# Float32r products of 512 columns issued as two of 256 in a two-block transformer kernel

## The chip, the cores and the metric

The kernel runs on one core of one Trainium2 chip. The metric is the device time of one execution in microseconds. Before the change it is 1270.01 us, the median of three runs (1269.93 to 1270.71).

## What is computed

The reference takes 512 tokens of width 1024 and sends them through two blocks, all in float32. The first block has an input projection, a short convolution branch, a gated delta rule branch with 8 heads, two output projections, a mixing projection, and a convolutional feed-forward part of width 2816. The second block has another input projection, an indexer that selects keys for one attention, a forgetting attention, a pooling branch and an output projection. Cut to what matters here, which is the large products:

```python
h = rmsnorm(x, norm_mix_g);  proj = h @ w_in                       # 1024 -> 9232
y_a = short_conv_branch(bg, cg, xv, conv_a_w) @ w_a_out            # 1024 -> 1024
y_b = gdn_branch(q, k, v, z, a, b, ...) @ w_b_out                  # 1024 -> 1024
x = x + (sigmoid(ga) * y_a + sigmoid(gb) * y_b) @ w_o
h = rmsnorm(x, norm_ffn_g)
up = causal_dwconv(h @ w_up, ffn_conv_w)                           # 1024 -> 5632
x = x + (silu(gate) * val) @ w_down                                # 2816 -> 1024
z = rmsnorm(x', norm_g_2) @ w_in_2                                 # 1024 -> 3886
x = x' + concat(pool, dsa, fox) @ w_out_2;  out = rmsnorm(x, final_g_2)
```

## The kernel before, in words

Activations lie transposed in SBUF: features on the 128 partitions, the 512 tokens along the free dimension. A weight matrix is worked off in units. A unit is one block of 128 output columns of one matrix: 128 weight columns by up to 1024 input features, which is 8 tiles of 128 x 128 (the second feed-forward matrix has units of 5 or 6 tiles). SyncE loads the block into one of four buffers `raw`. For accuracy every float32 value is used as a sum of two rounded float32r values: ScalarE writes the rounded block `whi` (L1329), VectorE, or in a late stretch GpSimd, writes the rest `wlo = raw - whi` (L1818, L2756). Both have two buffers, and ScalarE may write one again only when the unit that read it two units ago is done (`unit_done`). The activations have been split the same way into slots of `act_a` and `act_b`.

TensorE runs the units one after another in `unit` (L816 to L837). It first waits for `split_ready`. For each of the kn feature tiles it issues three products into the same PSUM bank `gb[:, b, :]` of 128 x 512 float32: high weights by high activations, low weights by high activations, and high weights by low activations. The weight tile is the stationary operand and the 512 tokens of the slot are the moving one. So a unit of 8 tiles is 24 products. `whole` runs a unit without a pause. With `parts=4` the unit is cut into four parts, and between the parts TensorE issues small steps of the head in work: float32 products and transposes of 128 x 128 or smaller (`key_products` L925, `query_products` L933, `step` L943 to L1016) and, in the second block, those of the written plan (`beside`, L1207 attention scores, L1219 transposes, L1229 attention by values). The order is written out by hand in the loops of `head`, `ups`, `down` and over `Z_UNITS`. Other engines wait for the last product of a unit (`unit_done`) and read the bank.

Not made by `unit` are the thin products of the first projection (L880 to L882, a weight tile of 16 columns by 512 tokens) and the last projection (`products`, L1279, 192 products whose stationary tile is an activation and whose moving operand is 512 weight columns).

Of the kernel before, what the change touches and what calls it, by code (L numbers as in the profile page):

```python
# [5 lines left out]
P = 128  # L6
# [198 lines left out]
def hybrid_block_kernel(nc, x, norm_mix_g, w_in, conv_a_w, gdn_conv_w, gdn_A_log, gdn_dt_bias, gdn_norm_g,  # L205
                        w_a_out, w_b_out, w_o, norm_ffn_g, w_up, ffn_conv_w, w_down, norm_final_g,
                        w_in_2, norm_g_2, pool_w_2, pool_scale_2, fox_bf_2, w_out_2, final_g_2, out):
    with ExitStack() as ctx:
# [85 lines left out]
        def slot(n):  # L294
            return act_a[:, n, :] if n < SLOTS_A else act_b[:, n - SLOTS_A, :]
# [25 lines left out]
        gb = ctx.enter_context(nc.psum_tensor("gb", [P, 4, T], F32))  # L321
# [493 lines left out]
        def _(pe):  # L815
            def unit(n, i, b, k0, rhs_hi, rhs_lo, kn=KD, first=True, last=True, parts=1, ready=None, high=None, packed=False):  # L816


                pe.wait_ge(split_ready, n + 1)
                todo = []  # L820
                for k in range(kn):
                    hi = whi[:, i % 2, k * P:k * P + P]
                    lo = wlo[:, i % 2, k * P:k * P + P]
                    a, c = slot(rhs_hi + k0 + k), slot(rhs_lo + k0 + k)
                    todo += [(hi, a), (hi, c)] if packed else [(hi, a), (lo, a), (hi, c)]
                each = len(todo) // parts
                per = len(todo) // kn
                for m, (l, r) in enumerate(todo):
                    if high and m % per == 0:
                        pe.wait_ge(high[0], high[1] + m // per + 1)  # L830
                    if ready and m % per == (per - 1 if high else 0):
                        pe.wait_ge(ready[0], ready[1] + m // per + 1)
                    ins = pe.matmul(gb[:, b, :], l, r, start=(first and m == 0), stop=(last and m == len(todo) - 1))  # L833
                    if m == len(todo) - 1:
                        ins.then_inc(unit_done, 1)
                    if (m + 1) % each == 0:
                        yield  # L837

            def whole(*a, **k):
                for _ in unit(*a, **k):  # L840
                    pass
# [56 lines left out]
            for r in range((R_END + P - 1) // P):  # L898
                m = min(P, R_END - r * P)
                ins = pe.transpose(gd[:, 1, r * P:r * P + m], prow[0:m, r * P:r * P + P], ident[0:m, 0:m])  # L900
            ins.then_inc(par_turned, 1)
            for m, _ in enumerate(unit(N_B, N_B, 0, 0, YB_HI, YB_LO, parts=4)):
                if m == 0:
                    pe.wait_ge(ab_ready, 1)
                    for c in range(TC):
                        ins = pe.transpose(gd[:, 0, c * P:c * P + AB_COLS], ob[0:AB_COLS, c, :],
                                           ident[0:AB_COLS, 0:AB_COLS])
                    ins.then_inc(ab_turned, 1)
                elif m == 2:
                    pe.wait_ge(par_ready, 2)  # L910
                    norm_spread(0)
# [106 lines left out]
            def head(h, peeled):  # L1018
                for s in range(8):
# [14 lines left out]
                    if peeled:  # L1034
                        u = unit(N_B + 8 * h + s, N_B + s, s % 4, 0, YB_HI, YB_LO, parts=4)
                    else:
                        u = unit(N_B + 8 * h + s, N_B + s, s % 4, 0, H_HI, H_LO, parts=4,
                                 ready=(h_ready, 0) if s == 0 else None)
# [232 lines left out]
            def products(i, c):  # L1271
                n, k = N_W + i, W_ORDER[i]
                hi = act_a[:, MIX_HI + k, c * P:c * P + P]
                lo = act_a[:, MIX_LO + k, c * P:c * P + P]
                for half in range(2):
                    wh = whi[:, n % 2, half * T:half * T + T]
                    wl = wlo[:, n % 2, half * T:half * T + T]
                    for m, (l, r) in enumerate(((hi, wh), (lo, wh), (hi, wl))):
                        ins = pe.matmul(place(c, half), l, r, start=False, stop=(i == KD - 1 and m == 2),  # L1279
                                        skip_group_check=True)  # L1280
                    if i == KD - 1 and (half == 1 or c == TC - 1):
                        ins.then_inc(tile_done, 1)
                return ins
# [16 lines left out]
            for i in range(2, KD - 2):  # L1300
                pe.wait_ge(split_ready, N_W + i + 1)
                pe.wait_ge(m_lo, i + 1)
                for c in range(TC):
                    ins = products(i, c)
# [1490 lines left out]
```

## Time and profile before

| | |
|---|---|
| median of three runs | 1270.01 us |
| span of the profiled execution, first to last instruction | 1268.4 us |
| TensorE products, records and busy time | 6633, 1253.7 us (99%) |
| TensorE weight loads, records and busy time | 6633, 1007.2 us (79%) |
| VectorE, ScalarE, GpSimd busy | 832.6, 578.6, 223.9 us |
| DMA, mean rate | 103 GB/s |

Times are in microseconds unless marked ns. PE is TensorE's products and PEld its weight loads, which overlap the products. L833 is line 833 of the kernel. A group of instructions is told by line, engine, operation, output<-inputs and shape. The recorded duration of a product reaches from its start to its modelled end and overlaps the next product's, so durations of products do not add up to time, and the distance between two starts is the time that a product takes. The profile has no own duration of the execution beside its span; the median of the runs is 1.6 us above it.

### The profile page before, as it was taken

Reading aid. Unit: us, or ns where it says so; the run is one execution under the profiler, and the core shown is the slowest. Engines: PE = TensorE matmul, PEld = TensorE weight load, DVE = VectorE, ACT = ScalarE, POOL = GpSimd, SP = SyncE. Lnnn points to the kernel's source line nnn. Section 1 sums busy time; section 2 is a strip of 40 time slices with the busy share of each in tenths; the row PEclk is TensorE's granted clock in tenths of the full one; section 3 lists DMA queues with packets and bytes.
Section 4 is the critical chain, followed back from the end, with each engine's and each line's share of the span. In section 5 each row is a group of like instructions: output and inputs, shape, how many; then the busy total and the mean of one; then the engine's idle time right before and its main releaser. Section 6 shows DMA issues by size and latency. Waiting matters only on the chain.

```text
span 1268.4 us, 20147 instructions
## 1 busy us (share of the span) xinstructions
PE 1253.7 (99%) x6633; PEld 1007.2 (79%) x6633; DVE 832.6 (66%) x1705; ACT 578.6 (46%) x1049; POOL 223.9 (18%) x476
## 2 busy tenths in 40 slices
PE   8999999999999999999999999999999999999998
PEld 6787878878788788888888888888888767777776
DVE  6978777787676843444477773367765686794743
ACT  5664545545455432223344442244444455666632
POOL 2603314032140400001300000000004124440021
PEclk9999999999999999999999999999999999999999
DMA  6345263453534433333233323433224334333221
GB/s 182 84 117 136 75 155 88 120 124 83 141 94 120 125 92 108 99 99 100 83 100 99 99 73 90 118 100 99 81 79 113 102 108 126 83 84 100 80 70 67
DMA packets 283492, 130.01 MB, mean 103 GB/s; under 512 B 77296, under 2 KB 276271, under 8 KB 283445
## 3 DMA queue, kind: packets, MB, share of 16 engines
q1 hardware_dynamic: 283445, 129.42, 37.3%
q8 instruction: 25, 0.41, 0.1%
q14 instruction: 22, 0.18, 0.0%
HBM read 119.34 MB, written 10.06 MB: 102 GB/s over the span
## 4 chain that ended last, share of the span: by engine, by line
PE 95%; DVE 2%; issue 1%; ACT 1%; DMA 0%; SPq 0%; POOLq 0%; DVEq 0%; POOL 0%; ACTq 0%
PE gb L833 82%; PE gb L1279 2%; PE gd L1279 1%; PE gd L1229 1%; PE gd L1219 1%; PE gd L1207 1%; PE gd L925 1%; PE gd L933 1%; PE gd L1005 1%; PE gd L1016 1%; PE gd L994 0%; PE gd L993 0%; PE gd L1012 0%; PE gb L1207 0%; PE gd L1186 0%
## 5 line engine op out<-in xcount | busy, mean ns | idle before, releaser
L833 PE MATMUL gb<-act_a,whi 128*128 128x512 f32 x2656 | 888.8, 398 | 0.3 <-DVE wlo L1818 0.2
L833 PEld LDWEIGHTS gb<-act_a,whi 128*128 128x128 f32 x2656 | 498.9, 188 | 112.0 <-issue 9.9
L833 PE MATMUL gb<-act_a,wlo 128*128 128x512 f32 x1408 | 548.9, 390 | 0.0
L1818 DVE TENSOR_TENSOR wlo<-raw,whi 128x1024 fp32r<-128x1024 f32 (+1 forms) x197 | 235.8, 1197 | 134.6 <-ACT whi L1329 132.5
L1329 ACT ACTIVATE whi<-raw 128x1024 fp32r<-128x1024 f32 (+1 forms) x210 | 216.1, 1029 | 216.9 <-PE gb L833 191.7
L833 PEld LDWEIGHTS gb<-act_a,wlo 128*128 128x128 f32 x1408 | 265.1, 188 | 48.2 <-issue 0.5
L833 PE MATMUL gb<-act_b,whi 128*128 128x512 f32 x432 | 152.5, 393 | 0.0
L833 PEld LDWEIGHTS gb<-act_b,whi 128*128 128x128 f32 x432 | 81.1, 188 | 17.3 <-DVE qc L2112 0.4
L2711 POOL TENSOR_TENSOR zs<-zs,ca 128x512 f32<-128x512 f32 x3 | 4.2, 1395 | 321.3 <-ACT ca L1332 321.3
L833 PE MATMUL gb<-act_b,wlo 128*128 128x512 f32 x128 | 49.9, 390 | 0.0
L2666 POOL TENSOR_TENSOR Ue<-Ue,elt 128x60 f32<-128x60 f32 (+14 forms) x120 | 45.0, 375 | 9.4
L2676 POOL TENSOR_TENSOR rr<-ss,eps_one 128x4 f32<-128x4 f32 x8 | 1.6, 201 | 234.8 <-DVE ss L2003 234.8
L2663 POOL TENSOR_TENSOR elt<-Ti,Ue 128x60 f32<-128x60 f32 (+14 forms) x120 | 37.6, 314 | 27.9 <-DVE Ti L1939 13.5
L2756 POOL TENSOR_TENSOR wlo<-raw,whi 128x1024 fp32r<-128x1024 f32 x13 | 31.2, 2400 | 23.6 <-ACT whi L1329 23.6
L1424 ACT ACTIVATE ob<-gd,hc 128x128 f32<-128x128 f32 x24 | 8.8, 368 | 54.2 <-DVE Rr L2059 54.2
L2323 DVE TENSOR_TENSOR Yb<-gb,Vt 128x512 f32<-128x512 f32 x22 | 15.2, 691 | 24.7 <-PE gb L833 24.7
L2694 POOL TENSOR_TENSOR zs<-zs,ca 128x512 f32<-128x512 f32 x3 | 5.6, 1857 | 134.3 <-ACT ca L1332 134.3
L2362 DVE TENSOR_TENSOR xT<-xT,gb 128x512 f32 (+1 forms) x16 | 11.0, 687 | 26.9 <-PE gb L833 26.9
L833 PEld LDWEIGHTS gb<-act_b,wlo 128*128 128x128 f32 x128 | 24.1, 188 | 4.5
L2448 DVE MAX8 small<-selb 128x8 f32<-128x256 f32 (+2 forms) x48 | 26.4, 549 | 0.4
L2449 DVE MATCH_REPLACE8 selb<-small,selb 128x256 f32<-128x256 f32 (+2 forms) x48 | 26.0, 543 | 0.0
L2112 DVE SCALAR_TENSOR_TENSOR kc<-gb,hw,kc 128x511 f32<-128x511 f32 (+2 forms) x24 | 18.0, 748 | 7.7 <-ACT kc L1445 7.1
(487 smaller groups left out, 1497.3 us busy)
## 6 DMA issues: line engine op xcount, KB each, us to landing
raw<-in_w_in_dram SPq DMA_DIRECT2D x102, 512.0 KB, 3.7
raw<-in_w_up_dram SPq DMA_DIRECT2D x44, 512.0 KB, 3.6
raw<-in_w_down_dram SPq DMA_DIRECT2D x16, 384.0 KB, 3.1
raw<-in_w_down_dram SPq DMA_DIRECT2D x16, 320.0 KB, 3.0
raw<-in_w_a_out_dram SPq DMA_DIRECT2D x8, 512.0 KB, 4.2
raw<-in_w_b_out_dram SPq DMA_DIRECT2D x8, 512.0 KB, 3.5
raw<-in_w_o_dram SPq DMA_DIRECT2D x8, 512.0 KB, 3.4
raw<-in_w_out_dram SPq DMA_DIRECT2D x8, 512.0 KB, 3.5
```

Of the source, the lines that this page charges most:

```text
L833: ins = pe.matmul(gb[:, b, :], l, r, start=(first and m == 0), stop=(last and m == len(todo) - 1))
L925: ins = pe.matmul(gd[:, 3, c * P:c * P + P], KT[:, c, :], KT[:, c, :], start=True, stop=True)
L1279: ins = pe.matmul(place(c, half), l, r, start=False, stop=(i == KD - 1 and m == 2), skip_group_check=True)
L1329: sc.activation(whi[:, i % 2, 0:k * P], raw[:, i % 4, 0:k * P], ACT.Copy).then_inc(hi_ready, 1)
L1818: dve.tensor_tensor(wlo[:, i % 2, 0:k * P], raw[:, i % 4, 0:k * P], whi[:, i % 2, 0:k * P].bitcast(F32), ALU.subtract).then_inc(split_read ...
L2112: ins = dve.scalar_tensor_tensor(dst[:, a:T], gb[:, at, 0:T - a], hw[:, 4 * b + 3 - a:4 * b + 4 - a], dst[:, a:T], ALU.mult, ALU.add)
L2323: dve.tensor_tensor(scaled[s], gb[:, 2 * q + s, :], flat(Vt), ALU.mult).then_inc(up_scaled, 1)
L2448: link(dve.max(small[:, 0:8], v))
L2449: link(dve.match_replace(v, small[:, 0:8], v, TAKEN))
L2663: pool.tensor_tensor(elt[:, :, 0:n], row_at(m), Ue[:, :, m:m + 1].to_broadcast([P, TC, n]), ALU.mult).then_inc(el_used, 1)
L2666: pool.tensor_tensor(Ue[:, :, m + 1:E], Ue[:, :, m + 1:E], elt[:, :, 0:n], ALU.subtract).then_inc(el_done, 1)
L2756: pool.tensor_tensor(wlo[:, n % 2, :], raw[:, n % 4, :], whi[:, n % 2, :].bitcast(F32), ALU.subtract).then_inc(split_ready, 1)
```

## The change

Every product of `unit` is issued as two. The first takes tokens 0 to 255 and writes columns 0 to 255 of the bank, the second takes tokens 256 to 511 and the other columns. Both have the same stationary tile. The start flag stands on the first half of the first product only, since it concerns the bank as a whole, and the group check of the compiler is turned off for these instructions. The waits stand ahead of the first half. The increment of `unit_done` is on the second half of the last product. Thin products, last projection and small steps stay as they are.

```diff
--- before.py
+++ after.py
@@ -830,7 +830,10 @@
                         pe.wait_ge(high[0], high[1] + m // per + 1)
                     if ready and m % per == (per - 1 if high else 0):
                         pe.wait_ge(ready[0], ready[1] + m // per + 1)
-                    ins = pe.matmul(gb[:, b, :], l, r, start=(first and m == 0), stop=(last and m == len(todo) - 1))
+                    for half in range(2):
+                        cols = slice(half * 2 * P, half * 2 * P + 2 * P)
+                        ins = pe.matmul(gb[:, b, cols], l, r[:, cols], start=(first and m == 0 and half == 0),
+                                        stop=(last and m == len(todo) - 1), skip_group_check=True)
                     if m == len(todo) - 1:
                         ins.then_inc(unit_done, 1)
                     if (m + 1) % each == 0:
```

## Rows read from the trace of the kernel before

**Rows 1.** The page: busy time, granted clock in 40 slices, chain that ended last.
```profile
PE 1253.7 (99%) x6633; PEld 1007.2 (79%) x6633; DVE 832.6 (66%) x1705; ACT 578.6 (46%) x1049; POOL 223.9 (18%) x476
...
PEclk9999999999999999999999999999999999999999
...
PE 95%; DVE 2%; issue 1%; ACT 1%; DMA 0%; SPq 0%; POOLq 0%; DVEq 0%; POOL 0%; ACTq 0%
PE gb L833 82%; PE gb L1279 2%; PE gd L1279 1%; PE gd L1229 1%; PE gd L1219 1%; PE gd L1207 1%; PE gd L925 1%; PE gd L933 1%; PE gd L1005 1%; PE gd L1016 1%; PE gd L994 0%; PE gd L993 0%; PE gd L1012 0%; PE gb L1207 0%; PE gd L1186 0%
```

**Rows 2.** Groups by form: shapes, count | busy us, mean ns | idle before.
```profile
L833 PE MATMUL gb<-act_a,whi 128*128 128x512 f32 x2656 | 888.8, 398 | 0.3 <-DVE wlo L1818 0.2
L833 PE MATMUL gb<-act_a,wlo 128*128 128x512 f32 x1408 | 548.9, 390 | 0.0
L833 PE MATMUL gb<-act_b,whi 128*128 128x512 f32 x432 | 152.5, 393 | 0.0
L833 PE MATMUL gb<-act_b,wlo 128*128 128x512 f32 x128 | 49.9, 390 | 0.0
...
L833 PEld LDWEIGHTS gb<-act_a,wlo 128*128 128x128 f32 x1408 | 265.1, 188 | 48.2 <-issue 0.5
```

**Rows 3.** Chain that ended last, in order of time: start, us, what.
```profile
463.11 163.24 PE gb L833 x720
...
636.11 351.17 PE gb L833 x1548
```

**Rows 4.** Waits of TensorE and ScalarE: total us, times, longest.
```profile
PE gd L870 <- DMA gate<-in_x_dram: 4.5, 1, 4.5
...
ACT whi L1329 <- PE gb L833: 191.7, 114, 4.4
```

**Rows 5.** Timeline of TensorE around 111 us: start, us, engine, line, count.
```profile
110.77 0.44 PE L943 MATMUL gd<-Tp,Lp 32*32 32x16 f32 x32
...
111.14 0.19 PEld L833 LDWEIGHTS gb<-act_a,whi 128*128 128x128 f32 x1
111.25 0.19 PEld L833 LDWEIGHTS gb<-act_a,wlo 128*128 128x128 f32 x1
```

**Rows 6.** Busy time by stretch, L933 alone: stretch, us, PE, PEld, clock, DMA.
```profile
102.90:104.40 1.50, 1.05 (x8) 0.90 (x8) 1.00 0.00 0
```

**Rows 7.** Line 933: durations, minimum/median/maximum in ns.
```profile
L933 PEld LDWEIGHTS gd<-QT,KT x64: 187/192/192, 49.5 to 424.7; 128*128 128x128 f32 x64
L933 PE MATMUL gd<-QT,KT x64: 270/275/275, 49.7 to 424.8; 128*128 128x128 f32 x64
```

**Rows 8.** Timeline of the weight loads of the same eight passes.
```profile
103.08 0.30 PEld L933 LDWEIGHTS gd<-QT,KT 128*128 128x128 f32 x2
...
103.53 0.30 PEld L933 LDWEIGHTS gd<-QT,KT 128*128 128x128 f32 x2
```

**Rows 9.** Groups by form of L1229, plain float32, 256 and 128 columns.
```profile
L1229 PE MATMUL gd<-ob,Vt 128*64 128x256 f32 x6 | 1.8, 379 | 0.0
...
L1229 PE MATMUL gd<-pT,Vt 128*64 128x128 f32 x6 | 1.1, 272 | 0.0
```

**Rows 10.** Timeline around 22 us: four transposes.
```profile
22.47 0.60 PE L854 MATMUL gd<-ident,rr 128*128 128x128 f32 x4
```

**Rows 11.** Timeline around 10 us: thin products and one of their loads.
```profile
9.92 0.39 PE L881 MATMUL gb<-act_b,wlo 128*16 128x512 f32 x1
...
10.84 0.40 PE L882 MATMUL gb<-act_b,whi 128*16 128x512 f32 x1
...
9.69 0.10 PEld L881 LDWEIGHTS gb<-act_b,wlo 128*16 128x16 f32 x1
```

**Rows 12.** Timeline around 123 us: two products of L833, six apart.
```profile
122.42 0.39 PE L833 MATMUL gb<-act_a,wlo 128*128 128x512 f32 x1
...
123.81 0.39 PE L833 MATMUL gb<-act_a,wlo 128*128 128x512 f32 x1
```

**Rows 13.** Busy time by stretch, L833 alone, with the DMA share (0.98).
```profile
122.00:124.20 2.20, 2.20 (x11) 1.65 (x9) 1.00 0.98 267
```

## The prediction

> **What bounds the kernel.** Four views, in this order. First the shares of busy time with the chain of waits [rows 1]: TensorE is busy for 1253.7 of 1268.4 us, the chain that ended last is 95% TensorE, and 82% of it is the one line that the change edits, L833. The granted clock is 9 or more in all 40 slices, the 2.4 GHz level. Then the groups of instructions [rows 2]: L833 issues 2656 + 1408 + 432 + 128 = 4624 products and has 0.3 us of idle time before them in all. Each has a weight load of its own, recorded at 188 ns on a second row that overlaps the products. The recorded 390 ns of a product are not its cost, since products overlap too. The cost is the distance from start to start, and the chain in order of time gives it without rounding [rows 3]: 720 products in 163.24 us are 226.72 ns each, 1548 in 351.17 us are 226.85 ns. I take 226.7. At 2.4 GHz that is 544 cycles for 512 columns, so 213.3 ns of columns (one a cycle) and 13.4 ns of something else. This remainder is what the prediction turns on. A new bank every 24 products adds nothing to it.
>
> Last the waits [rows 4]: TensorE waits 4.5 us for the first input and for little else, while ScalarE stands idle for 191.7 us until a product of L833 is done, before it may overwrite a weight buffer. It is the last wait almost everywhere, and it falls on the engine that is not the bound. So a change in the pitch of L833 goes into the time one for one, 4624 times. If products slow down, all others gain slack. If they speed up by a few per cent, that idle time covers it.
>
> **The change part by part.**
> *Removed:* 4624 products of 512 columns. *Added:* 9248 products of 256 columns, and as many weight loads, since each product in the trace has its own load (6633 of each [rows 1]). The same 512 columns pass for every product of before: the column time of 213.3 ns stays. What the change costs is 4624 x (2p - 226.7 ns), p being the pitch of a half product. The trace has no float32r product that is not 512 wide, so p must be bounded.
>
> *Below, by the weight load.* Each half needs a full 128 x 128 load. Two places show how close loads can follow. After a step the array is empty: L833's first load starts at 111.14, the next, which in this trace starts when the product before it does, at 111.25 [rows 5], so load to product is 0.11 us. And the plain float32 products of L933, four to a call, leave eight records in 1.05 us [rows 6]: each runs in two passes. A pass has the load of a full tile, 187 to 192 ns as here [rows 7], and 128 columns at half rate: 128 more columns of such a pass lengthen it by 379 - 272 = 107 ns, two cycles a column [rows 9]. So a pass is a full load beside 256 cycles, or 106.7 ns, which is the very shape of a half product. The last of the eight lasts 0.275, so they are (1.05 - 0.275)/7 = 0.111 us apart; loads at 103.08 and 103.53 with four steps between give 0.1125 [rows 8]. So a load and 256 cycles overlap nearly completely and p is not below 0.111. That end is 2 x 111 - 226.7 = -4.7 ns, a gain of 4624 x 4.7 = 21.7 us.
>
> *From the product's side.* 106.7 ns of columns plus a share of the 13.4 ns. If this is paid per product, p = 106.7 + 13.3 = 120.0. If most of it is paid per column, a small fixed part remains, for which the transposes stand: four of L854 in 0.60 us are (0.60 - 0.272)/3 = 0.109 us apart for 106.7 ns of columns [rows 10], 2.6 ns fixed. Then 226.7 - 2.6 = 224.1 halves to 112.0, and p = 114.6.
>
> *Which of the two.* The products with a 16-column weight [rows 11] run at the same pitch as L833 ((10.84 - 9.92)/4 = 0.23 us) though their loads last 0.10 instead of 0.19 us: so the remainder is not the weight load showing through, and it will not vanish because of how loads lie. The plain passes of L933 have 4 to 6 ns over their columns [rows 6, 8] and the transposes 2.6 [rows 10], L833 has 13.4 with twice as many cycles. A cost per column would have to be one of the float32r stream alone, for which I see no reason in the rows; a longer hand-over from one product to the next is simpler, and 32 cycles is a round number for one. The recorded duration speaks a little the other way: a pass of 106.7 ns of columns lasts 272 ns [rows 9], which leads to 272 + 106.7 = 378.7 for 512 columns of L833, and the trace has 389 to 390 [rows 2], as if the columns themselves ran longer. I take the fixed cost, p = 120.0, and keep both ends.
>
> The Trainium skill ("TensorE: Matmul & The Clock Gate", Wait — 56ns, not 53.3ns?) puts the back-to-back distance at the columns over 2.4 GHz plus a constant 2.5 ns, measured alike at 128 and 512 columns. By it alone an extra product costs 2.5 ns, 4624 of them 11.6 us, close to the rival of the cost per column; but the trace has 13.4 ns where it has 2.5, so for this data type it does not hold as it stands, while that the surplus is a constant would support my choice.
>
> *Issue.* Twice as many instructions a microsecond must be issued. The cover is wide: 32 records of L943, 16 products, lie within 0.44 us behind a wait [rows 5], so TensorE's queue delivers a product in at most 0.44/16 = 0.028 us, and a half lasts four times that. At nothing. *Waits and signals.* The waits stand ahead of the first half, the signal of the end on the last half: as many as before, and PSUM is complete when the last column has passed, as before. At nothing. The start flag is on the very first half of a group only; the second half's columns begin as unwritten. Nothing in time. *Reads.* Weight loads read twice as much. In a stretch with the DMA engines 98% busy the pitch was (123.81 - 122.42)/6 = 0.2317 [rows 12, 13], 5 ns more than elsewhere; should the doubled loads collide likewise, 4624 x 5 ns = 23 us. The passes of L933 have that density of loads and show nothing of it [rows 6]. At nothing, and inside the range.
> *Not touched:* L1279 with its 192 products, the thin products, all float32 steps, DMAs, and the 14.7 us of TensorE idle time.
>
> **Sum.** 4624 x (240.0 - 226.7) = 61.5 us. The profiled execution's span is 1268.4, so 1329.9; the median of the runs is 1270.0, 1.6 us more than the span (start and end around it), which gives 1331.5 us, 4.8% slower.
>
> **The rivals.**
> 1. *The remainder belongs to the columns.* p = 114.6, 2p = 229.2, 4624 x 2.5 = 11.6 us: 1281.6. With the 5.8 ns of the other reading [rows 8] as the fixed part, p = 106.7 + 5.8 + (13.4 - 5.8)/2 = 116.3 and 4624 x 5.9 = 27: 1297. For it: the long recorded duration. Against: no other row shows columns slower than their rate.
> 2. *The other side, the load is all that counts.* If the 13.4 ns is spent at a point where a waiting next load keeps the array fed, half products run at the pitch of the plain passes, 111 ns [rows 6], and the product gets cheaper: 1270.0 - 21.7 = 1248; at 0.1125 (-1.7 ns a product, 7.9 us) it is 1262. The point from which it decides is p = 113.35 ns. For it: the same load and the same 256 cycles run at 111 to 112.5 there. Against: those passes are of the other stream, and the thin products keep their 13 to 17 ns with next to no load.
> 3. *Load and remainder in series.* If the hand-over can only begin when the load is through, p = 111 + 13.3 = 124.3, 2p = 248.6, 4624 x 21.9 = 101.3: 1371. For it: now load and columns end together, where before the load had 100 ns to spare. Against: the first product after a step starts 0.11 us after its load, with no 13 ns behind it [rows 5].
> 4. *Half products fall to the slow rate.* Were a narrower product handled as plain float32 (two passes of half rate), a half would cost 2 x 111 = 222 ns, 4624 x 217 = 1005 us: 2275. No row speaks for it but that all products of this type here are 512 wide.
> 5. *The second load is left out, the tile being the same.* Then the load no longer bounds p, but with a fixed cost it is 120 all the same and with a hand-over that only a load causes it is 226.7 for the pair: 1270. No two products in a row share a tile today, so no row excludes it; that loads equal products in number [rows 1] says little.
>
> The Trainium skill (same page, Measured speedup vs the span model) states that a weight load overlaps a running product only if their row groups differ, which speaks against this change: loads would stand bare. The trace contradicts it: all of L833 is of one row group, and its loads of 188 ns lie within a pitch of 226.7 together with 213.3 ns of columns [rows 2, 3]. I give it no part.
>
> **How the numbers follow.** Fixed cost 0.48; columns 0.26; load alone 0.11; in series 0.08; second load left out or nothing changed 0.04; slow rate 0.03. Predicted is the likeliest, 1331.5. The range goes from 1260, which takes in the half of rival 2 nearest to no change, to 1372, the series case; about 0.1 stays out. The likeliest's own range is 1320 to 1345, for the 5 ns of collisions and a fixed part somewhat below the whole. Beyond 0.2% (2.5 us), which is what a measurement of this kernel can tell from no change: faster 0.11, within 0.05, slower 0.84.
>
> **What would show it.** TensorE and its loads should have 6633 + 4624 = 11257 records each. In the chain in order of time a clean stretch of half products should have 120 ns each (114 to 117 for rival 1, 111 to 113 for 2, 124 for 3). Recorded duration of a half: 389 - 106.7 = 282 ns, if the surplus is fixed, about 277 if it goes with the columns. The load row should be busy above 95%, since loads of 188 ns follow at 120. Idle time before ScalarE's L1329 should grow by most of the 61 us. The 2.4 GHz level should stay. I am wrong if p in the long stretches of L833 is under 118 or over 122.

## The result and the profile after

The change makes the kernel slower: 1321.01 us (1321.00 to 1321.08) against 1270.04 us, a ratio of 1.0401 with a 95% interval of [1.0388, 1.0414]. That is 51.0 us or 4624 x 11.0 ns, where 61.5 us were forecast.

The page after, in answer to [rows 1]:

```profile
PE 1306.7 (99%) x11257; PEld 1261.0 (96%) x11257; DVE 836.3 (63%) x1705; ACT 578.1 (44%) x1049; POOL 219.6 (17%) x476
...
PEclk9999999999999999999999999999999999999999
...
PE 96%; DVE 2%; issue 1%; ACT 1%; DMA 0%; SPq 0%; POOLq 0%; DVEq 0%; POOL 0%; ACTq 0%
```

Products and loads both grew by 4624. TensorE stays the bound at the same clock level. The loads' row went from 79% to 96%. The chain in order of time has the pitch (the distance from the start of one product to the start of the next), in answer to [rows 3]:

```profile
91.26 14.40 PE gb L835 x120
...
477.98 172.80 PE gb L835 x1440
...
660.81 371.74 PE gb L835 x3096
```

172.80/1440 = 120.0 ns and 371.74/3096 = 120.1 ns: a product of before now takes 240.0 in place of 226.7 ns. ScalarE's idle time behind L835 grew by 41 us (191.7 before, [rows 4]):

```profile
ACT whi L1332 <- PE gb L835: 232.6, 132, 4.7
```

The durations of line 835, minimum/median/maximum:

```profile
L835 PEld LDWEIGHTS gb<-act_a,wlo x2816: 187/192/193, 72.0 to 1262.6; 128*128 128x128 f32 x188
L835 PE MATMUL gb<-act_a,wlo x2816: 277/283/288, 72.1 to 1262.8; 128*128 128x256 f32 x188
```

**Where the rise is smaller.** The two long stretches, 2268 products, rose by 30.1 us, 13.3 ns each. The seven heads between the piece at 89.48 (before; 91.26 after) and the long stretch took 463.11 - 89.48 = 373.63 us before and 477.98 - 91.26 = 386.72 after: 13.1 us for 1344 products, 9.7 ns each. The chain shows why. Before, in runs of six products between two small steps:

```profile
126.26 0.22 PE gd L1016 x2
126.48 1.39 PE gb L833 x6
127.87 0.22 PE gd L993 x2
```

And the same place after:

```profile
129.48 0.22 PE gd L1019 x2
129.70 1.43 PE gb L835 x12
131.13 0.22 PE gd L996 x2
```

Before, such a product took 1.39/6 = 231.7 ns, 5 ns more than in a long run. After it is 1.43/6 = 238.3. So here the change costs 7 ns a product.

The recorded starts before show where the 5 ns lie. These three are of the run of 60 products that begins at 89.48, with seven steps from the first to the second and ten from there to the third:

```profile
89.55 0.40 PE L833 MATMUL gb<-act_a,wlo 128*128 128x512 f32 x1
...
91.18 0.40 PE L833 MATMUL gb<-act_a,whi 128*128 128x512 f32 x1
...
93.45 0.39 PE L833 MATMUL gb<-act_a,whi 128*128 128x512 f32 x1
```

The pitch is 1.63/7 = 233 ns at first and then 2.27/10 = 227 ns. So only the first products of a run are slower, whatever its length: the 60 take 13.65 us, 0.05 more than 60 x 226.7 ns. The 120 halves that stand there after the change take 14.40 us (the piece at 91.26 above), just 120 x 120.0. The 1344 products of the seven heads stand in 126 such runs, of 6, 12, 30 and 60. At 13.3 ns each they would have cost 17.9 us. They cost 4.8 us less, 38 ns for each run.

### The profile page after: what moved, and what is told of

Same layout as the page of the kernel before. It is cut to its first block, busy times and chain, and to the rows that moved or that the text cites. A ratio compares the mean times of both kernels' runs of the same rounds, so it can differ in the third digit from the quotient of the medians.

```text
span 1319.3 us, 29395 instructions
## 1 busy us (share of the span) xinstructions
PE 1306.7 (99%) x11257; PEld 1261.0 (96%) x11257; DVE 836.3 (63%) x1705; ACT 578.1 (44%) x1049; POOL 219.6 (17%) x476
## 4 chain that ended last, share of the span: by engine, by line
PE 96%; DVE 2%; issue 1%; ACT 1%; DMA 0%; SPq 0%; POOLq 0%; DVEq 0%; POOL 0%; ACTq 0%
PE gb L835 83%; PE gb L1282 2%; PE gd L1282 1%; PE gd L1232 1%; PE gd L1222 1%; PE gd L1210 1%; PE gd L1008 1%; PE gd L936 1%; PE gd L928 1%; PE gd L1019 1%; PE gd L996 0%; PE gd L1015 0%; PE gd L997 0%; PE gb L1210 0%; PE gd L987 0%
## 5 line engine op out<-in xcount | busy, mean ns | idle before, releaser
L835 PE MATMUL gb<-act_a,whi 128*128 128x256 f32 x5312 | 918.8, 286 | 0.1
L835 PEld LDWEIGHTS gb<-act_a,whi 128*128 128x128 f32 x5312 | 751.2, 191 | 11.9 <-issue 9.6
L835 PE MATMUL gb<-act_a,wlo 128*128 128x256 f32 x2816 | 566.8, 283 | 0.0
L835 PEld LDWEIGHTS gb<-act_a,wlo 128*128 128x128 f32 x2816 | 438.2, 191 | 0.0
L835 PE MATMUL gb<-act_b,whi 128*128 128x256 f32 x864 | 157.8, 284 | 0.0
L835 PEld LDWEIGHTS gb<-act_b,whi 128*128 128x128 f32 x864 | 126.8, 192 | 0.3
L835 PE MATMUL gb<-act_b,wlo 128*128 128x256 f32 x256 | 51.5, 283 | 0.0
L2669 POOL TENSOR_TENSOR Ue<-Ue,elt 128x60 f32<-128x60 f32 (+14 forms) x120 | 38.8, 323 | 9.4
L835 PEld LDWEIGHTS gb<-act_b,wlo 128*128 128x128 f32 x256 | 39.8, 191 | 0.0
L1757 ACT ACTIVATE pT<-gd 128x512 f32<-128x512 f32 (+3 forms) x24 | 10.5, 437 | 31.0 <-PE gd L1222 17.8
```

The source lines that it names most:

```text
L835: ins = pe.matmul(gb[:, b, cols], l, r[:, cols], start=(first and m == 0 and half == 0), stop=(last and m == len(todo) - 1), skip_group_ch ...
L2669: pool.tensor_tensor(Ue[:, :, m + 1:E], Ue[:, :, m + 1:E], elt[:, :, 0:n], ALU.subtract).then_inc(el_done, 1)
```

## The experiments

Experiments that leave part of the work out (fewer tokens, fewer output features, narrower numbers) were run once each, and their pitches come from one trace. In the five kernels of the tables the first block's whole products serve as a gauge: a run of 60 takes 13.61 to 13.65 us in each, as before.

Three theories. **A**, the forecast's: every float32r product costs 13.3 ns beyond one cycle a column. **B** (the load): the 120 ns at 256 columns comes from the weight load beside it. **C** (rival 1's part): the surplus, that is the 13.4 ns over one 2.4 GHz cycle a column, goes with the columns, so a half streams in 113.4 ns.

**Only 384 of the 512 tokens.**
```diff
-                    ins = pe.matmul(gb[:, b, :], l, r, ...)
+                    cols = slice(0, T if m == 0 else 384)
+                    ins = pe.matmul(gb[:, b, cols], l, r[:, cols], ...)
```


> Every product of a unit but its first (4421 of 4624) takes 384 tokens only; the last 128 tokens are left out. Nothing is split, so loads are as many as before and lie even further apart than 106.7 ns. Theory A (a fixed cost of 13.3 ns on each float32r product, beside one cycle a column): pitch in long stretches 160.0 + 13.3 = 173.3 ns. Theory C (the surplus goes with the columns, 226.7 x 384/512 and 2.6 ns fixed): 170.7 ns. Theory B (at 256 columns the pitch of 120 was set by the weight load, and the 13.3 ns at 512 columns is something else): says nothing firm here, 170 to 174. The run's time falls by up to 4421 x 53.3 ns = 236 us, less where another engine becomes the bound.

The timeline of line 834, two products with eleven steps from start to start:
```profile
741.71 0.34 PE L834 MATMUL gb<-act_a,whi 128*128 128x384 f32 x1
...
743.62 0.34 PE L834 MATMUL gb<-act_b,whi 128*128 128x384 f32 x1
```
1.91/11 = 173.6 ns, A's number (173.3) and not C's (170.7). The granted clock was 1.00 from 741 to 744 us; over the whole execution its mean was 0.976. The run took 1185.28 us, with VectorE's `wlo` now waited for. Taken alone this run would have confirmed A.

**Uneven split, 384 and 128.**
```diff
+                    for at, to in ((0, 384), (384, 512)):
+                        ins = pe.matmul(gb[:, b, at:to], l, r[:, at:to], ...)
```


> Every product is split unevenly, 384 and 128 tokens, all computed. Theory A with no bound from the load: 173.3 + 66.7 = 240.0 ns a product, as the even split, 1321 us. Theory A with a load floor L for the product that follows the short one: 173.3 + L. With L = 111 (plain float32 passes) 284.3 ns, 4624 x 57.6 = 266 us over before, 1536. Theory B (load 106.7 + hand-over 13.3, L = 120): 293.3 ns, 4624 x 66.6 = 308 us, 1578. If a 128-column product falls to the slow rate (two passes of 111 ns): 395 ns, over 2000 us.

1529.84 us, ratio 1.2042 [1.2022, 1.2062]. The chain, single loads, and two products in a row:
```profile
550.74 206.35 PE gb L834 x1440
```
```profile
799.93 0.19 PEld L834 LDWEIGHTS gb<-act_a,whi 128*128 128x128 f32 x1
800.04 0.19 PEld L834 LDWEIGHTS gb<-act_a,whi 128*128 128x128 f32 x1
800.22 0.19 PEld L834 LDWEIGHTS gb<-act_a,whi 128*128 128x128 f32 x1
...
800.79 0.22 PE L834 MATMUL gb<-act_a,wlo 128*128 128x128 f32 x1
800.85 0.39 PE L834 MATMUL gb<-act_a,whi 128*128 128x384 f32 x1
```
206.35/720 = 286.6 ns a product. The loads follow alternately at 0.11 and 0.18 us. The products' recorded starts lie otherwise, at 0.06 and 0.23 us, and the 384-column part is recorded at 0.39 us where the run before had 0.34. Its record seems to begin 0.05 us ahead of its columns, which is an inference. So here neither row of starts gives the pitch of one part, and only the sum is safe. 286.6 less 173.6 leaves 113 ns for the 128 columns, more than twice their 53.3: there is a load floor of 111 to 113 ns and no slow rate. B's 120 behind the load alone is out.

**A 64-column weight tile, split evenly.**
```diff
+                    w = P if m == 0 else P // 2
+                    for at in (0, 2 * P):
+                        ins = pe.matmul(gb[0:w, b, at:at + 2 * P], l[:, 0:w], r[:, at:at + 2 * P], ...)
```


> The even split, but every product of a unit except its first uses only 64 of the 128 weight columns (half the output features are left out), so a weight load takes 53 ns less (135 instead of 188 ns recorded, as the 64-column loads of before). Theory A (13.3 ns belong to the product): the pitch of a half stays 120.0 ns, the time stays 1321 within 2. Theory B (the load sets 120): the half falls to 106.7 + a few ns, 110 to 113, and the time by some 8996 x 8 ns = 70 us to 1250.

1270.99 us: twice the instructions at the time of before. The chain and the durations:
```profile
462.06 163.83 PE gb L835 x1440
```
```profile
L835 PEld LDWEIGHTS gb<-act_a,wlo x2816: 132/135/139, 70.3 to 1212.6; 128*64 128x64 f32 x188
L835 PE MATMUL gb<-act_a,wlo x2816: 274/277/285, 70.4 to 1212.7; 128*64 128x256 f32 x188
```
With the 60 products of full tiles taken out at 120, (163.83 - 7.20)/1380 = 113.5 ns, half of 226.7 within 0.2 ns and not 120. A product lasts 277 ns, what the prediction gave for a cost that goes with the columns; the 283 of the change is that plus what the full load does to it. This run overturns A: a second product costs nothing of its own. What it left out is one half of the weight load, but also one half of the output columns. The tables below tell the two apart.

**Another order, few tiles twice in a row** (the three left halves of a feature tile, then the three right ones).
```diff
+                turns = [(m, half) for k in range(kn) for half in range(2) for m in range(per * k, per * k + per)]
+                for at, (m, half) in enumerate(turns):
```


> All 9248 half products, but in another order: for each feature tile first the three left halves, then the three right halves, so that two products in a row never share a weight tile. Theory A: nothing depends on the tile being the same, 120.0 ns a half and 1321 us within 0.2%. Rival (a repeated tile is recognised and its load shortened or skipped in part): the pitch rises above 120, time above 1324. If instead writing the same tile again collides, it falls below 1318.

1321.3 us, ratio 1.0403 [1.0386, 1.0421], and the same long piece:
```profile
478.06 172.80 PE gb L836 x1440
```
The edit does a little less than its expectation says. The last left half and the first right half of a feature tile both take its high weights, so one half in six still follows its own tile, where it was every second one. With two thirds of the repeats gone the time has not moved, and in both kernels every half has a load record of its own. That the tile repeats is neither used nor punished, which closes rival 5.

**A table of pitches, in three kernels.** Each stretch without steps has its own form; the first product of a unit stays whole, so pieces of the chain between two such products can be counted.
```diff
+                    if form[0] == "plain" or (m == 0 and first):
+                        ins = pe.matmul(gb[:, b, :], l, r, **part)
+                    elif form[0] == "c2":
+                        for at, to in ((0, 512),):
+                            ins = pe.matmul(gb[0:64, b, at:to], l[:, 0:64], r[:, at:to], **part)
...
```


> A table of pitches with a weight load that is out of the way: in the stretches without steps all products but a unit's first use 64 of 128 weight columns and a number of tokens that differs by stage (the rest is left out): output projections and gates 512, mixing projection 264, first part of the up projection 2 x 240, second part 2 x 192, down projections 384. Theory D (6.67 ns for each started block of 256 columns, which the earlier runs suggest with 113.3 at 256 and 173.6 at 384): 226.7; 123.3; 106.7 each; 86.7 each; 173.3. Theory A (13.3 ns fixed, and 64-column weights save 6.67 of it): 220.0; 116.7; 106.7; 86.7; 166.7. Theory C (17/16 of a cycle a column): 226.7; 116.9; 106.3; 85.0; 170.0. 512 and 264 tell them apart.

```profile
559.93 5.29 PE gb L840 x23
...
604.98 2.77 PE gb L843 x23
...
640.92 4.92 PE gb L846 x46
...
741.35 6.07 PE gb L852 x35
...
785.49 4.09 PE gb L849 x46
```
With 64-column tiles: 512 columns 230.0 ns, 264 120.4, 240 107.0, 384 173.4, 192 88.9 (the only whole piece of that stage, whose other pieces are broken up by waits). 512 is nowhere near A's 220. Theory D of the expectation has 384 and 240 right and misses 512 and 264 by 3 ns each.

> The same table with full weight tiles, parts of the tokens left out: output projections and gates 448, mixing projection 264, first part of the up projection 2 x 240, second part 2 x 192, down projections 320. With a surcharge of 13.3 over 256 columns: 200.0, 123.3, then the load floor, then 146.7. The floor is the question for 2 x 240 and 2 x 192: 113.3 ns if the load alone sets it (106.7 + 6.67, as behind the short product of the uneven split), 120.0 if the float32r load with its hand-over takes 120 whatever streams beside it, 111 if it is that of plain float32 passes.

```profile
562.49 4.67 PE gb L840 x23
...
577.37 2.76 PE gb L843 x23
...
644.24 5.15 PE gb L846 x46
...
737.96 5.13 PE gb L852 x35
...
792.00 5.11 PE gb L849 x46
```
With full tiles: 448 203.0 ns, 320 146.6, 240 112.0, 192 111.1, 264 120.0 to 121.3 (448 and 264 lie 3 ns off the expectation, on either side). The load floor is 111 ns, that of the plain float32 passes [rows 6]. So at exactly 256 columns neither the floor (111) nor the columns (113.5) explains 120.0.

Side by side the two tables say what the width of the tile does. At 384 and 264 columns it does nothing (173.4 and 173.6, 120.4 and 120.0 to 121.3), at 512 the full tile is even the faster one, and at 256, 240 and 192 it costs 6.5, 5.0 and 22 ns. If fewer output columns were what saves time, they would save it at 264 and 384 too. So it is the load, and in these tables only where it is about as long as the product's columns or longer. They also settle theory C. The surplus over one cycle a column is 7 ns at 240 and 256 columns with a light load, 10 at 264, 13.3 to 13.6 at 320 and 384, 16 at 448 and 13.4 to 17 at 512. It is neither a constant nor a share of each column.

> The same stages with the upper halves of the words read as bfloat16 (so with less of the numbers, and parts of the tokens left out), full weight tiles: output projections and gates 512, mixing projection 264, first part of the up projection 2 x 256, second part 4 x 128, down projections 384. If the surcharge belongs to float32r: 213.3 + 2 to 3 ns, 112.5, 109 each, 384 at 162.5, and the pitch of a split product equals that of a whole one within 3 ns. If it belongs to any product with a load in front: 226.7, 123.3, 120 each, 173.3. 4 x 128: at the weight load, 56 to 113 each.

```profile
541.90 5.19 PE gb L842 x23
...
602.46 2.70 PE gb L845 x23
...
639.98 5.23 PE gb L848 x46
...
745.81 5.94 PE gb L854 x35
...
861.59 5.30 PE gb L851 x92
```
```profile
L848 PEld LDWEIGHTS gb<-act_a,whi 128*128 128x128 bf16 x720 | 69.5, 97 | 12.0
```
512 columns 225.7 ns, 264 117.4, 2 x 256 113.7 each, 384 169.7, 4 x 128 57.6 each, with full tiles whose load is recorded at 97 ns instead of 188. Here the surplus grows with the columns (4.3 ns at 128, 7.0 at 256, 12.4 at 512), for operands that are not float32r, but lie 4 bytes apart as well. And splitting is nearly free: 227.4 against 225.7. Of the expectation for a surcharge of float32r alone, the free split came true and the small surplus did not; of the other, 226.7 at 512 nearly came true, and 120 at 256 did not.

**The width of the tile at 2 x 256 columns**, in two kernels with the stages exchanged.
```diff
+                        for at, to in ((0, 256), (256, 512)):
+                            ins = pe.matmul(gb[0:120, b, at:to], l[:, 0:120], r[:, at:to], **part)
```


> Even split, width of the weight tile differing by stage (other output features left out): output projections and gates 120 of 128 columns, mixing projection 112, first part of the up projection 96, second part 32, down projections full tiles but 2 x 248 tokens. A load takes width/1.2 ns, 6.7 ns less for each 8 columns. Theory load tie (120 comes from load and columns ending in the same moment, and goes as soon as one of them is a little shorter): 113.3 ns at 120, 112, 96 and 32 columns, and 113.3 or 110 at 2 x 248. Theory load + hand-over (13.3 behind the load): 113.3 at 120 columns, then the columns' own 113.3. Theory A (fixed 13.3 for tiles of over 64 columns): 120.0 at 120, 112 and 96, 113.3 at 32, and 116.7 at 2 x 248.

```profile
561.26 5.43 PE gb L840 x46
...
600.43 5.21 PE gb L843 x46
...
640.57 5.34 PE gb L846 x46
...
771.31 7.94 PE gb L852 x70
...
828.91 5.42 PE gb L849 x46
...
861.84 5.22 PE gb L849 x46
```
118.0 ns at 120 columns of weights, 113.3 at 112, 116.1 at 96, 113.5 at 32, and 113.4 to 115 at full width with 248 tokens. Two stages have a second level. The first whole unit at 32 columns takes 5.42 us, 117.8 ns a product, where the later ones take 5.22 to 5.23. The first one at 112 columns, the piece at 583.88, takes 5.42 us too. So a product of one and the same form can run at either pitch for a whole unit.

> The widths of the weight tile again at 2 x 256 tokens (other output features left out), with the stages exchanged: output projections and gates 96 columns (116.1 ns when it stood in the up projection), mixing projection 104, up projection 120 (118.0 in the output projections) and 112 (113.4 in the mixing projection), down projections 124. If the pitch goes with the width: 116, something between 113.4 and 116, 118, 113.4, and 118 to 120 for 124. If it goes with the stage (what other engines do then): 118, 113.4, 116.1, 113.5 in that order, whatever the width.

```profile
560.08 5.34 PE gb L840 x46
...
605.06 5.43 PE gb L843 x46
...
640.73 5.40 PE gb L846 x46
...
773.72 8.39 PE gb L852 x70
...
838.81 5.21 PE gb L849 x46
```
96 gives 116.1 again, 104 gives 118.0, 120 117.4 to 118, 112 113.3 again, 124 117.2 to 120. So it goes with the width more than with the stage, and not in order of the width. A load that merely ends a little too late would have given a pitch that falls steadily with the width. Theory tie as I had put it fails: what load and columns do to each other near 256 columns costs 0 to 6.5 ns, and its mechanism stays open. That one unit with a 32-column tile runs at 117.8 says that the length of the load is not all of it, and 112 columns at 113.3 say the same from the other side.

**Two other splits of the whole computation.**
```diff
+                    for at, to in ((0, 264), (264, 512)):
```


> The whole computation, every product split into 264 and 248 tokens. Theory tie (a half of 256 columns streams in 113.4 ns, and 120.0 only comes about where a full float32r load of 111 ns runs beside it and ends nearly with it): 264 columns 120.2, 248 columns 113.4 to 115.0, together 234 to 235 ns against 240.0 for the even split. Long stretches at 234.5, the time by 4624 x 5.5 = 25 us under the even split: 1296 (1290 to 1302). Theory A (13.3 ns on each product): 240.0 and 1321 within 2.

1307.12 us, ratio 1.0289 [1.0272, 1.0306]; the long stretch is at 365.86/1548 = 236.3 ns:
```profile
655.60 365.86 PE gb L834 x3096
```
Moving eight tokens from one half to the other wins 14 us over the even split. A has no room for that. The 1296 us of the tie were too low by 11 us, and outside its range: a product was expected at 234.5 ns and took 236.3. Which of the two parts is the longer one is not shown.

> The whole computation, split into 288 and 224 tokens. Theory tie: 288 columns between 264's 120.2 and 320's 146.7, 133 in the middle, 224 columns on the load floor at 111 to 112, together 244.5: longer than the even split by 4.5 ns, 1341. Theory A: 240.0, 1321, as every split in two whose parts stay above the load. So theory tie has its best split between, and A has none.

1345.63 us, ratio 1.0593 [1.0575, 1.0610], 245.5 ns a product (380.00/1548), 5 us over the expectation, which had put the 224-column part on the load floor and 288 columns at 133. No split tried is faster than the whole product, 226.7, so nothing here beats the kernel before.

**Only units without parts are split.**
```diff
+                    for half in range(2) if parts == 1 else (None,):
```


> Only the 1104 products of units without parts (gates, output projections, mixing and down projections) are split, evenly; the 3520 of the other units stay whole. If the rise of 13.3 ns holds for products in long runs: 1104 x 13.3 = 14.7 us, 1284.7 us (1.1% over before), which leaves 36.3 us or 10.3 ns each for the others, the small steps among them eating the difference. If all products pay the mean of 11.0 ns alike: 12.2 us, 1282.2.

1284.93 us, ratio 1.0115 [1.0098, 1.0131]: 14.6 us for 1104 products, 13.3 ns each. The other 3520 thus carry 51.0 - 14.6 = 36.4 us or 10.3 ns each. The prediction's 13.3 ns holds where products follow one another; the missing 10.5 us lie among the units with parts.

## Why the prediction was right, and where it was not

- *The bound and one for one.* Right. TensorE is still 99% busy, and none of its own waits grew by more than 0.1 us. Others did, ScalarE's by 41 us, and cost nothing.
- *p = 120.0 ns.* The number is measured to the digit in long stretches, but the reason for it was wrong. The step that failed is the choice between the two readings of the 13.4 ns ("I take the fixed cost"), and in it the inference from the thin products [rows 11]. They show that the surplus of a 512-column product is not the load; they say nothing about a 256-column one, where the load lasts as long as the columns. A product of 256 columns with a light load takes 113.5 ns, so its own surplus is 7 ns and not 13.3. The 6.5 ns more for each half come from the full float32r load beside it, 2 x 6.5 = 13 ns a product, by luck what a fixed cost would have given. That the load is the partner is shown by taking its width away; how it makes 6.5 ns of it is not. What the surplus itself is made of stays open: 13.3 at 320 and 384 columns looks like the fixed cost, 7 at 240 and 256 does not. The one row that spoke against me, the recorded 389 ns [rows 2], pointed to 277 ns for a half, which the light load has.
- *Below, by the load: 111 ns.* Right: 111.1 at 192 columns. What I left out is that load and columns of nearly one length disturb each other above either of their own times. The passes of L933 [rows 6, 8] have that shape and run at 111 to 112.5, so shape alone doesn't tell it. One reading behind the floor was loose: at 111 us [rows 5] the second load starts at 111.25, but the product before it is recorded from 111.14 and the next one only from 111.48. The 0.11 us there is the distance of two loads, as in the uneven split.
- *The sum, 61.5 us.* The term 4624 x 13.3 was mis-sized. 2268 products of the long stretches paid 13.3 ns, those of the seven heads 9.7, the rest 50.9 - 30.1 - 13.1 = 7.7 us over 1012 (the spans grew by 50.9), 7.6 ns. The 5 ns that I had put down to busy DMA engines [rows 12, 13] are in every run of six, busy or not, and do not add to the new cost. Here is such a run, and the stretch around it, in which the DMA engines are idle (share 0.00):

```profile
80.09 1.39 PE gb L833 x6
...
80.10:81.40 1.30, 1.30 (x7) 1.04 (x7) 0.38 (x2) 0.89 (x2) 0.00 (x0) 1.00 0.00 0
```

They belong to the first products of a run, and the halves do not have them: 4.8 of the 10.5 us that the forecast was too high come from this in the seven heads. What makes these products slow before the change stays open.
- *Rivals.* 1 is near for a half with a light load (114.6, measured 113.5), wrong at 384 columns (170.7, measured 173.6) and wrong in the total (1281.6). 2, the gain: half products do not reach 111. 3 (124.3) did not come. 4: a 128-column product does not fall to a slow rate. 5: closed by the changed order.
- *The rule on row groups.* The Trainium skill ("TensorE: Matmul & The Clock Gate", The mechanism, where the sentence stands, and not the section that the prediction names) says that a weight load overlaps a running product only if their row groups differ. The 64-column run has 4624 more loads at the time of before, 1270.99 us, so they are hidden within one row group, as the trace had said.
- *Issue.* Nothing, as forecast: the 64-column run issues as many instructions as the change in 1270.99 us.

## What to carry to other kernels

Cutting a float32r product with a full weight tile from 512 to 2 x 256 columns costs 13 ns of 227 in a long run and 7 to 10 between small steps, and in the long run the price is that of the second weight load, not of the second product: with a 64-column tile, or with bfloat16 operands whose load is recorded at 97 ns, the same cut was free within 2 ns. Keep the moving side well longer than the load (111 ns here); at 256 columns a few weight columns more or less change the pitch by several ns. A pitch at one size can't tell a fixed cost from one by column, and a forecast that hits the number may do so for another reason, so measure at two sizes and with the suspected partner made small.

## Not expected of the hardware

- Products take more than one 2.4 GHz cycle a column: 57.6 ns for 128, 113.7 for 256, 225.7 for 512 with bfloat16 read at a step of 4 bytes, and 113.5 for 256 (64-column tile), 226.7 for 512 (full tile) with float32r. In between, float32r is not smooth: 107.0 at 240, 120.0 to 121.3 at 264, 146.6 at 320, 173.4 at 384, 203.0 at 448.
- At 256 columns the pitch depends on the width of the weight tile without order: 113.5 (32 and 64), 116.1 (96), 118.0 (104), 113.3 (112), 118 (120), 117 to 120 (124), 120.0 (128). At 32 and 112 columns one unit each ran at 117.8 from end to end.
- Runs of six whole products between plain float32 steps take 231.7 ns each, 5 ns more than in long runs, whose first products are as slow. Halves of 256 columns do not show it.
